# First expert's up products in pairs of contraction tiles, and two gate-row steps placed later on VectorE

## What is computed

```python
mix, st_new = mixing_block(x, st, l, P, lb_all[l], pos0)
x = layer_norm(ALPHA * x + mix, ...)
if l % 2 == 0: ffn = swiglu(x, ffn_w1, ffn_w3, ffn_w2)      # 1024 -> 2816 -> 1024
else:          ffn = moe_swiglu(x, ...)                     # top 2 of 8 experts, 1024 -> 1408 -> 1024
x = layer_norm(ALPHA * x + ffn, ...)
```

## Time and profile before

| | us |
|---|---|
| median of 3 runs | 1006.69 (1002.21 to 1008.4) |
| profiled execution, its own time | 1004.63 |
| span of that execution | 1002.8 |
| PE busy | 986.8 (98%) |
| DVE / ACT / POOL busy | 504.6 / 193.0 / 81.8 |
| mean granted clock of PE | 0.996 |
| HBM traffic | 241.43 MB, mean 241 GB/s |

### The profile page before, as it was taken

One profiled execution on the slowest core, in us unless ns is written; L12 is line 12 of the kernel. 1 busy time (PEld: TensorE's weight loads), 2 busy tenths in 40 slices (PEclk: granted clock), 3 DMA queues, 4 the chain that ended last, 5 costly groups with the idle time before them and its releaser, 6 DMA issues.

```text
span 1002.8 us, 23772 instructions
## 1 busy us (share of the span) xinstructions
PE 986.8 (98%) x10688; PEld 789.7 (79%) x10688; DVE 504.6 (50%) x1032; ACT 193.0 (19%) x414; POOL 81.8 (8%) x105
## 2 busy tenths in 40 slices
PE   9999999999999999999999999999999999999995
PEld 6897877999999999998988779556666767667533
DVE  6888894764666654269878975430101201011135
ACT  1333333221111000044333241400000000000001
POOL 1110021600000000000000200230000020000020
PEclk9999999999999999999999999999999999999998
DMA  9427349214443155201233378899999999999982
GB/s 356 148 90 240 117 151 368 91 74 180 168 168 128 74 191 222 108 29 57 86 103 132 120 307 333 332 331 379 402 415 398 422 391 412 425 421 423 422 334 83
DMA packets 37498, 241.43 MB, mean 241 GB/s; under 512 B 5008, under 2 KB 8144, under 8 KB 17680
## 3 DMA queue, kind: packets, MB, share of 16 engines
q1 hardware_dynamic: 27280, 216.69, 55.3%
q0 software_dynamic: 6432, 19.43, 5.4%
q10 hardware_dynamic: 3680, 3.74, 1.2%
HBM read 228.60 MB, written 13.07 MB: 241 GB/s over the span
## 4 chain that ended last, share of the span: by engine, by line
PE 91%; DVE 4%; DMA 3%; ACT 1%; issue 1%; SPq 0%; DVEq 0%
PE ps L773 69%; PE ps L1378 15%; PE ps L1486 6%; DMA up_slots<-in_moe_w 3%; PE ps L776 1%; PE ps L1315 1%; DVE overlay L2506 0%; DVE small L2459 0%; ACT up_slots L1835 0%; ACT x L1835 0%; DVE tables L3096 0%; DVE x L2266 0%; ACT overlay L1835 0%; DVE overlay L2261 0%; DVE overlay L2464 0%
## 5 line engine op out<-in xcount | busy, mean ns | idle before, releaser
L773 PE MATMUL ps<-up_slots,mix_or_moe 128*32 128x352 f32 (+2 forms) x3248 | 238.8, 451 | 0.6 <-DMA up_slots<-in_moe_w 0.4
L773 PEld LDWEIGHTS ps<-up_slots,mix_or_moe 128*32 128x32 f32 (+2 forms) x3248 | 135.5, 111 | 96.3 <-issue 9.3
L773 PE MATMUL ps<-x,up_slots 128*128 128x144 f32 (+3 forms) x832 | 152.3, 336 | 0.0
L773 PEld LDWEIGHTS ps<-x,up_slots 128*128 128x128 f32 x832 | 124.7, 190 | 25.1 <-issue 8.8
L773 PE MATMUL ps<-overlay,tables 128*32 128x256 f32 (+4 forms) x1992 | 121.5, 375 | 0.0
L773 PEld LDWEIGHTS ps<-overlay,tables 128*32 128x32 f32 (+2 forms) x1992 | 91.6, 113 | 26.6 <-issue 2.4
L3135 DVE TENSOR_TENSOR mix_or_moe<-mix_or_moe,ps 128x352 f32<-128x352 f32 x24 | 11.2, 518 | 174.0 <-PE ps L773 174.0
L1378 PE MATMUL ps<-overlay,up_slots 128*128 128x144 f32 x704 | 91.7, 286 | 0.6 <-DVE overlay L2911 0.3
L1378 PEld LDWEIGHTS ps<-overlay,up_slots 128*128 128x128 f32 x704 | 88.3, 190 | 1.1 <-issue 0.8
L773 PE MATMUL ps<-up_slots 128*128 128x144 f32 (+2 forms) x768 | 87.1, 282 | 1.2 <-DVE up_slots L2540 1.0
L773 PEld LDWEIGHTS ps<-up_slots 128*128 128x128 f32 (+2 forms) x768 | 79.5, 186 | 5.3 <-DVE up_slots L2540 1.9
(11 more groups left out here) (379 smaller groups left out, 1010.5 us busy)
## 6 DMA issues: line engine op xcount, KB each, us to landing
up_slots<-in_moe_w SPq DMA_DIRECT2D x64, 1408.0 KB, 24.9
overlay<-in_moe_w SPq DMA_DIRECT2D x21, 1536.0 KB, 26.7
up_slots<-in_ffn_w SPq DMA_DIRECT2D x30, 1024.0 KB, 6.9
up_slots<-in_w_in SPq DMA_DIRECT2D x27, 1024.0 KB, 5.1
up_slots<-in_w_out SPq DMA_DIRECT2D x8, 1024.0 KB, 7.3
overlay<-in_moe_w SPq DMA_DIRECT2D x7, 1024.0 KB, 26.4
mix_or_moe<-in_states POOLq DMA_DIRECT2D x6, 512.0 KB, 7.3
expert_tokens<-in_shape_tables POOLq DMA_DIRECT2D x8, 384.0 KB, 7.6
```

The lines of the kernel that those rows point to most:

```text
L773: return pe.matmul(o, lhsT, rhs, start=start, stop=stop)
```

## The change

In `first_up`, the halves become pairs: for each pair of contraction tiles, PE goes through the three groups and takes two products of each. The number of products, their operands and the sums are the same. Two DVE instructions with their waits, an addition into `N0S` and a copy of the input gate's row, go from the end of `gate_rows` to the start of `gate_maxima`, so in both layers they run after `operands(0)`, `boundary(2)` and `operands(1)`.

```diff
             def first_up():
-                for k0 in (0, KH):
+                for k0 in range(0, KT, 2):
                     for g in range(NG):
                         if k0 == 0:
                             pe.wait_ge(*((S["first_xe"], g + 1) if g < 2 else (S["xe_done"], 1)))
-                        for k in range(k0, k0 + KH):
+                        for k in range(k0, k0 + 2):
                             if g == 0 and k % 2 == 0:
                                 pe.wait_ge(w1_full[k // 2], 16)
                             last = up_product(0, k, W1, g, U1_BANKS[0][g])
...
                     link(cp(rtmp, rlf))
                     link(v.memset(rtmp[:, SEQ:T:DSEQ], NEG))
+
+                def gate_maxima():
                     link(tt(N0S[:, 48:56], rlf[:, SEQ:T:DSEQ], M0[:, l, :], AD))
                     link(cp(rlf, rli))
-
-                def gate_maxima():
                     link(tt(rlf[:, SEQ:T:DSEQ], rli[:, SEQ:T:DSEQ], N0S[:, 48:56], MX))
```

## The result

The changed kernel takes 1009.75 us (median of 20 runs, 1007.02 to 1014.28), the kernel before 1007.04 us (20 runs beside them, 1001.56 to 1011.4). The ratio on record, which is not that of the medians, is 1.0048, 95% interval 1.0031 to 1.0065; the two medians alone give 1.0027, the two means 1.0035. So it is slower by 0.3 to 0.5 per cent. The forecast was 1015.1. The profiled execution takes 1008.2 us, span 1006.3, with a mean clock of 0.993; that is 3.57 us more than before's.

A forecast was written before the change was run, and what follows sets the result against it. PE, 91% of the chain of waits, was taken as the bound. 1004.63 + 10.5 (stand 9.2, clock 2.1, far end -0.4, gate rows -0.35) gave 1015.1 us; whole range 1003.5 to 1021, its own 1011 to 1019.

The forecast's parts named there:

- The hold of 1.87 us: Release of expert 1's first w1 load, assumed 1.87 us late again behind product 6, so issued at 646.2.
- The busy DMA engines: Around the first expert, the DMA engines were said to have no idle time that an earlier load could fill.
- The first packets: Expert 1's first weight packets were to come about 1.5 us behind the load's issue, at 647.7.
- The collision: Expert 0's scatter: 365 packets left, alternating one for one with weights, end at 662.6 and not 652.2, 10.4 us later.
- Reading back: POOL's reads of expert 1's slots and DVE's transposes also go 10.4 us later; tokens there at 679.5.
- When PE wants them: PE wants expert 1's tokens at 670.3, after expert 0's w3 products, and stands until they come: +9.2 us.
- The clock: Behind PE's stand before expert 1, PE works 4.1 us at half speed: +2.1 us.
- half a collision: Rival: load issued at 647 to 648, 10 to 16 packets per engine meet weights, 1007 to 1011 us; chance 0.13.
- The far end: At the last expert's w3 weights, PE comes later and no longer waits: -0.4 us.
- The gate rows: Two moved DVE steps: 0.5 us gained in layer 1, 0.15 lost in layer 0; -0.35 us in sum.
- No collision: Rival: first load held until about 648.5, or the scatter keeps its share; 1003.9 to 1004.3 us; chance 0.32.
- full collision: Rival: no hold of expert 1's first load, PE stands 15 us, 1020 to 1023 us; chance 0.08.

The follow-up runs named there:

- the five traces named above: The trace of the kernel before that the prediction read (span 1004.63 us) and the four traces of changed kernels on chip 1.
- e5_product12: Changed kernel, with expert 1's first weight load released behind product 12 and not product 6: 1001.44 us, ratio 0.9959.
- e7_w2_later: Changed kernel, with the second of two early w2 loads put behind expert 1's four w1 loads: 1001.91 us, ratio 0.9954.
- before_again: Kernel before, unchanged, 12 more runs on chip 4: six in 1000.72 to 1003.66 us or within, six in 1006.14 to 1010.94; traced execution in the upper group.
- e2_gates: Kernel before with only the two gate-row steps moved, the first expert in halves as before: 1006.19 us, ratio 1.0002.
- e9_before_w2_later: Kernel before, with the second of two early w2 loads put behind expert 1's four w1 loads: 1005.36 us, ratio 1.0013.
- e3_scatter_first: Changed kernel, but SP waits for all six scatters before issuing expert 1's first weight load: 1006.46 us, ratio 0.9993.
- e8_wait64: Changed kernel, with expert 1's first load held until the first four of six scatters have landed: 1005.67 us, ratio 0.9991.

## Why the prediction was right, and where it was not

The direction, the mechanism and the place were right. The size was not: the change was forecast at +10.5 us and is +3.6 between the two traces and +2.7 between the medians; the time came out 5.4 us below the forecast, outside its own range of 1011 to 1019 and inside the whole one of 1003.5 to 1021. Part of that is the base, an execution with two delays of its own.

**The base.** The hold of 1.87 us that I read in the earlier trace rows and carried over belongs to the five traces named above, and is absent after. Against the kernel before on chip 4, where there is none, the first load is 646.89 - 643.78 = 3.1 us earlier: four products (2.37) and 0.74 that the whole stage begins earlier. The prediction took 646.2; its sign was a load at 644 to 647.

**The busy DMA engines.** They are not 90% busy from 602 us on, as is said above the rows: in the page's slices that begins at about 652 us, with 80 to 89% from 602, and from 630 to 635 the share is only 0.48. In the stretch that the argument is about, 640 to 670 us, it is 0.97 to 1.05, so the step that an earlier load finds no idle time there holds.

**The first packets.** Forecast 1.5 us behind the issue, found 3.4: issued at 643.78, first at 647.22. The forecast of 647.7 was nearly right by luck: two errors cancelled. Nor is the lag one figure: with the scatter under way it is 1.0 to 3.5 us in eleven traces (1.67 in the one that the prediction read).

**The collision.** 365 packets left at 647.7 were forecast, 323 are left at 647.2 (259 of them rows), 20 per engine, and they alternate with weights one for one. The Trainium skill (DMA: Bandwidth & Descriptors, Queues, rings and completion order) has an engine drain a packet of some 9 to 17 descriptors before it turns; the distance of 0.57 us from one scatter record to the next, one weight record and one row, shows a turn after each record that the trace counts; if such a record is the page's descriptor or its packet, no trace here says. A pair took 0.57 and not 0.65 us, since a weight record takes 0.42 and not the 0.51 that was worked out from the earlier trace rows, and it began 0.5 us earlier with fewer left: 20 x 0.57 = 11.5 us, the last row ends at 658.9, and DVE goes on at 659.88, not at 662.6.

**Reading back.** I let it take its old 15.0 us from the residual to the transposes; it took 12.6. With the scatter's 2.8 us this makes the tokens 5.3 us earlier than forecast; the transposes begin at 672.52, where the sign was "behind 675".

**When PE wants them.** Forecast 670.3, found 668.6: the stage began 0.8 us earlier and the stand of 1 us is absent. So the stand is 5.66 us and not 9.2: 5.3 less for the tokens, 1.7 more for PE's being there earlier. This is the term that was mis-sized.

**The clock.** Forecast 2.1 us, by the trace 1.7, by the experiment with a busy PE about 1.8. The forecast took it from a stretch at the end of the kernel, and the rival "half a collision" had a stand of 3 to 7 us as mostly too short for the clock; 5.66 us were not.

**The far end.** I gave it 0.4 us, as all that earlier loads can give. From the start of the last w3 (955.54 and 961.18) to PE's last long group (986.82 and 989.69) the trace after is 5.64 - 2.87 = 2.8 us shorter. 0.65 of it is the w3 stage with its wait, and this is the term of the forecast. The other 2.1 are not the change's: they are the idle time in the last w2 products that the five traces named above have and the nine others have not, two of which (e5_product12, e7_w2_later) reach these products as early as before, at 970.3 and 969.4. The first group of them takes 9.18 us in the trace that the prediction read, 7.05 after, and 7.05 in the same kernel before on chip 4. Here are the one of before with its idle weight loads, before again, and after:

```profile
970.39 9.18 PE L773 MATMUL ps<-up_slots,tables 128*32 128x512 f32 x64
975.79 0.16 PEld L773 LDWEIGHTS ps<-up_slots,tables 128*32 128x32 f32 x4 [1.00 <-issue]
977.24 0.18 PEld L773 LDWEIGHTS ps<-up_slots,tables 128*32 128x32 f32 x8 [1.28 <-issue]
```

```profile
974.98 7.05 PE L773 MATMUL ps<-up_slots,tables 128*32 128x512 f32 x64
```

```profile
961.18 14.38 PE L773 MATMUL ps<-up_slots,mix_or_moe 128*32 128x352 f32 x192
975.38 7.05 PE L773 MATMUL ps<-up_slots,tables 128*32 128x512 f32 x64
```

The sum closes: -0.8 - 1.0 + 5.7 + 1.7 = +5.6 at the last w3, then -2.8, is +2.8 us at 989.7, and 0.7 more behind it. But the stand of 1.0 us near 647 and the 2.1 us in the last w2 belong to the one execution of before that was traced. Without these 3.1 us the change costs 3.6 + 3.1 = 6.7 us, near the 6.4 that the pairs alone lose against before's lower heap on chip 3, and this is what the forecast of 10.5 is to be held against.

**The gate rows.** Right in both layers, in the traces; no run's time can show 0.3 us. PE's wait of 0.47 us is gone in layer 1 (to be set against the earlier trace rows); from a level product of layer 0 that lies behind the moved steps (53.94 before) to level 0 of layer 1 (464.42 before) are 410.2 to 410.5 us in the five traces without the edit and 409.7 to 409.9 in seven of the nine with it (410.2 and 410.5 in the others). In layer 0 the stretch from level 1 to level 2, with the gate columns in it (41.07 to 46.69 before, 40.77 to 46.51 after), grew by 0.12 us, forecast 0.15.

```profile
463.62 1.11 PE L773 MATMUL ps<-up_slots 64*128 64x64 f32 x16
```

**The rivals.** "No collision" had 0.32. It is what a third to two fifths of before's executions do on chips 3 and 4, and what all do on chip 1, but not the changed kernel: none of its 20 runs, nor of the 12 of the pairs alone, lies below 1007. By its number the result lies in "half a collision" (0.13; 1007 to 1011, a stand of 3 to 7 us), by its release in "full collision" (0.08; no hold, the load at 644.3), which had a stand of 15 us. The release came as early as there, but the first packets followed it by 3.4 us and not by under 2, and met 323 records and not 548. What I had no case for is that before is itself divided. That is why the 6 to 7 us that the change loses against its undisturbed executions show as only 2.7 in the medians.

Open stays what makes PE stand on chip 1; what divides the kernel before (the two traces of the slower course with halves, before_again and e2_gates, have a late engine, but the run that was to remove it, e9_before_w2_later, fell on a chip without that heap); and a further group at 1011 to 1014 in the changed kernel (8 of 20 runs, clock 0.991 or 0.992), with the pairs alone (3 of 12) and with PE kept at work (4 of 12): no trace shows one.

## What to carry to other kernels

A load that is released early is not free if a transfer with small packets is under way and something waits for its last packet: each of those packets then waits for a large one, and the engine that is last decides. Put that one release off until the small transfer is nearly through (here by six products, 0.4% below before where before collides), or clear the queue ahead of it, but don't wait for its end, since idle DMA time comes back at the last weights. Where the runs of a kernel fall in two heaps, one trace shows only one of its courses; set a difference between two traces against the same stretch in further traces of either kernel before it is put down to the change.

## What the runs showed of the hardware

- From SP's issue to the first weight packet: 0.95 us on idle engines (e3_scatter_first, 652.23 to 653.18; 0.95 and 0.94 in e8_wait64 and e9_before_w2_later), 1.0 to 3.5 us with the scatter on them (3.44 after, 643.78 to 647.22; 1.67 before).
- Two queues with work on an engine take turns by packet: a scatter row of 4 KB every 0.57 us beside weight packets of 11.3 KB (0.42 us each), every 0.37 us beside packets of 5.6 KB (0.22 us each).
- A transfer over 16 engines ends with the last of them: before_again has 557 of 576 rows started at 651, and the last at 657.04.
- A stand of 5.66 us put PE's clock to the low level during the stand and for 3.4 us of work behind it; the same stretch with 5.54 us of products in it and 0.91 us of waiting left it at the full level.
- In four of four traces on one chip PE stands about 1 us near 647, a signal comes over 1 us late, and the last w2 products take about 2 us more; in eight of eight on two others there is none of this, for the kernel before as for changed ones.
